# Recurrent sublayer: its recurrent columns projected first, the taps beside the other projections, the last operations tile by tile

## The reference, cut to what matters

```python
def rglru_block(h, w_in, conv_w, conv_b, w_r, b_r, w_i, b_i, lam, w_out):
    gate, xb = jnp.split(h @ w_in, 2, axis=-1)
    xp = jnp.pad(xb, ((0, 0), (CONV_W - 1, 0), (0, 0)))
    xc = conv_b + xp[:, 0:S] * conv_w[0]
    for tap in range(1, CONV_W):
        xc = xc + xp[:, tap:tap + S] * conv_w[tap]
    xblk = xc.reshape(B, S, LRU_BLOCKS, LRU_BLOCK_W)
    r = jax.nn.sigmoid(jnp.einsum('bsnk,nkj->bsnj', xblk, w_r).reshape(B, S, D_RNN) + b_r)
    i = jax.nn.sigmoid(jnp.einsum('bsnk,nkj->bsnj', xblk, w_i).reshape(B, S, D_RNN) + b_i)
    log_a = -LRU_C * r * jax.nn.softplus(-lam)
    a = jnp.exp(log_a)
    b = jnp.sqrt(-jnp.expm1(2.0 * log_a)) * (i * xc)
    _, hs = lax.associative_scan(_lin_rec_combine, (a, b), axis=1)
    y = jax.nn.gelu(gate) * hs
    return y @ w_out
```

## Time and profile before

| what | value |
|---|---|
| median of 3 runs | 2405.94 us (2405.05 to 2410.12) |
| profiled execution | 2406.02 us, its span 2404.4 us |
| PE busy | 2234.8 us, 93% of the span |
| PEld busy | 2038.2 us, 85% |
| DVE busy | 1634.5 us, 68% |
| ACT busy | 1216.3 us, 51% |
| POOL busy | 366.2 us, 15% |
| chain that ended last | PE 82%, DVE 7%, ACT 4%, issue 3%, DMA 3% |
| mean granted clock of PE | 0.96 |

### The profile page before, as it was taken

One profiled execution on the slowest core, in us unless ns is written; L12 is line 12 of the kernel. 1 busy time (PEld: TensorE's weight loads), 2 busy tenths in 40 slices (PEclk: granted clock), 3 DMA queues, 4 the chain that ended last, 5 costly groups with the idle time before them and its releaser, 6 DMA issues.

```text
span 2404.4 us, 37585 instructions
## 1 busy us (share of the span) xinstructions
PE 2234.8 (93%) x14486; PEld 2038.2 (85%) x14486; DVE 1634.5 (68%) x1943; ACT 1216.3 (51%) x1898; POOL 366.2 (15%) x513
## 2 busy tenths in 40 slices
PE   2999999999999994999998999998999699998998
PEld 2998987998899893899786998987988698877987
DVE  6767764767776846686787776775776776665654
ACT  2544545544553455553465554535544554565543
POOL 0111100111121103021101120800210121000210
PEclk9999989999999996999999999999999899999999
DMA  8788882688897961687765678512688378442562
GB/s 331 250 292 304 281 285 96 236 303 301 262 315 259 313 208 36 223 310 262 283 224 183 201 264 279 184 36 88 228 282 264 85 256 288 159 143 68 178 201 105
DMA packets 295522, 532.98 MB, mean 222 GB/s; under 512 B 10065, under 2 KB 185564, under 8 KB 295388
## 3 DMA queue, kind: packets, MB, share of 16 engines
q1 hardware_dynamic: 262396, 358.05, 45.3%
q0 software_dynamic: 32992, 173.09, 20.1%
HBM read 530.00 MB, written 1.11 MB: 221 GB/s over the span
## 4 chain that ended last, share of the span: by engine, by line
PE 82%; DVE 7%; ACT 4%; issue 3%; DMA 3%; SPq 0%; POOL 0%; DVEq 0%; ACTq 0%
PE bk L1344 12%; PE bk L1345 12%; PE bk L1346 12%; PE bk L1245 8%; PE bk L1243 8%; PE bk L1244 8%; PE bk L1395 3%; PE bk L1594 2%; DMA mod_raw<-in_ada_w 2%; DVE w_lo L1711 2%; PE bk L1288 1%; DVE mod_acc L1730 1%; PE bk L1231 1%; PE bk L1233 1%; PE bk L1232 1%
## 5 line engine op out<-in xcount | busy, mean ns | idle before, releaser
L1711 DVE TENSOR_TENSOR w_lo<-raw,w_hi 128x1024 fp32r<-128x1024 f32 (+5 forms) x720 | 833.0, 1185 | 512.7 <-ACT w_hi L791 511.4
L791 ACT ACTIVATE w_hi<-raw 128x1024 fp32r<-128x1024 f32 (+5 forms) x720 | 683.2, 976 | 683.0 <-PE bk L1245 335.7
L1344 PE MATMUL bk<-a_hi,w_hi 128*128 128x256 f32 x2332 | 664.5, 285 | 5.9 <-DVE a_lo L1796 5.9
L1345 PE MATMUL bk<-a_lo,w_hi 128*128 128x256 f32 x2332 | 663.0, 284 | 0.0
L1346 PE MATMUL bk<-a_hi,w_lo 128*128 128x256 f32 x2332 | 662.8, 284 | 0.0
L1344 PEld LDWEIGHTS bk<-a_hi,w_hi 128*128 128x128 f32 x2332 | 451.2, 194 | 7.1 <-DVE a_lo L1796 4.6
L1345 PEld LDWEIGHTS bk<-a_lo,w_hi 128*128 128x128 f32 x2332 | 451.1, 193 | 0.0
L1346 PEld LDWEIGHTS bk<-a_hi,w_lo 128*128 128x128 f32 x2332 | 450.9, 193 | 0.0
L1730 DVE SCALAR_TENSOR_TENSOR mod_acc<-mod_raw,cact,mod_acc 128x1536 f32<-128x1536 f32 x182 | 329.7, 1812 | 37.8 <-DMA mod_raw<-in_ada_w 22.8
L1245 PE MATMUL bk<-w_hi,hid_lo 128*128 128x512 f32 x832 | 327.5, 394 | 0.0
L1243 PE MATMUL bk<-w_hi,hid_hi 128*128 128x512 f32 x832 | 323.9, 389 | 3.7 <-DVE w_lo L1711 3.7
(11 more groups left out here) (341 smaller groups left out, 3180.6 us busy)
## 6 DMA issues: line engine op xcount, KB each, us to landing
raw<-in_ffn_w SPq DMA_DIRECT2D x128, 1024.0 KB, 5.5
mod_raw<-in_ada_w POOLq DMA_DIRECT2D x128, 768.0 KB, 6.1
raw<-in_ffn_w_gu SPq DMA_DIRECT2D x88, 1024.0 KB, 7.6
mod_raw<-in_mod_w POOLq DMA_DIRECT2D x80, 768.0 KB, 6.8
raw<-in_ffn_w_down SPq DMA_DIRECT2D x40, 1024.0 KB, 7.4
first_mod<-in_mod_w SPq DMA_DIRECT2D x16, 768.0 KB, 9.9
raw<-in_sb_w_qkv SPq DMA_DIRECT2D x12, 1024.0 KB, 7.1
raw<-in_conv_w_pw SPq DMA_DIRECT2D x12, 1024.0 KB, 5.4
```

The source lines that it names most:

```text
L791: ins = act.activation(o(w_hi[:, p % OPS, :]), r(raw[:, c % RAWS, :]), ACT.Copy)
L1344: pe.matmul(o, wh, a_hi[:, f, :], start=(f == 0), stop=False)
L1345: pe.matmul(o, wh, a_lo[:, f, :], start=False, stop=False)
L1711: ins = dve.tensor_tensor(o(w_lo[:, p % OPS, :]), r(raw[:, c % RAWS, :]), o(w_hi[:, p % OPS, :].bitcast(F32)), ALU.subtract)
```

## The change

Jobs 0 and 1 project recurrent tiles 0 to 7, job 2 gate tiles 0 and 1 and recurrent tiles 8 and 9, jobs 3 and 4 gate tiles 2 to 9. Job 2's two chunks take columns from two places, so each is loaded by two transfers of half the width; the first of each has a semaphore of its own (`mixed_landed`), for which ACT waits before it converts. The taps of DVE stand between the weight conversions of jobs 1, 2 and 3, in groups of four, four and two tiles. The gate matmuls begin in the banks of job 3, so the first four need not wait for ACT's eviction of job 4. The four last loops of DVE become one: round i makes product i, scan i - 1, Gelu product i - 2 and cast i - 3.

```diff
@@ -315,6 +315,7 @@
         prod_ready = sem("prod_ready")
         pos_landed = sem("pos_landed")
         pool_landed = sem("pool_landed")
+        mixed_landed = [sem("mixed_landed0"), sem("mixed_landed1")]
         pos_ready = sem("pos_ready")
         rope_read = sem("rope_read")
         rope_in = sem("rope_in")
@@ -380,6 +381,7 @@
             stages = stages[:stop]
         LAST_GROUP = max([0] + [h for z in stages for h in z["groups"]])
         st_pool = [z for z in stages if z["kind"] == "pool"]
+        st_lru = [z for z in stages if z["kind"] == "lru"]
         NPIECE = 2 * (stages[-1]["c"] + CHUNKS[stages[-1]["kind"]])
 
         act_base = [KD * (z["n"] + sum(y["kind"] == "conv" for y in stages[:z["n"]])) for z in stages]
@@ -541,7 +543,16 @@
                         plain(c + 12 + b, t["sb_w_o"][0], 4 * (b % 2), 4, 512 * (b // 2))
                 elif st["kind"] == "lru":
                     for b in range(10):
-                        plain(c + b, t["lru_w_in"][0], 4 * (b % 2), 4, b // 2 * 512)
+                        if b // 2 == 2:
+                            kt = 4 * (b % 2)
+                            sp.wait_ge(lo_ready, 2 * (c + b) + 2)
+                            for s in range(2):
+                                sp.dma_start(raw[:, (c + b) % RAWS, :].rearrange("p (k s m) -> p s k m", s=2, m=256)[:, s],
+                                             t["lru_w_in"][0][(b - 4) * 4 * P:(b - 3) * 4 * P, 2304 * s:2304 * s + 256]
+                                             .rearrange("(k p) m -> p k m", p=P))\
+                                    .then_inc(landed[(c + b) % RAWS] if s else mixed_landed[b - 4], 16)
+                        else:
+                            plain(c + b, t["lru_w_in"][0], 4 * (b % 2), 4, (1280, 1792, None, 256, 768)[b // 2])
                         if b == 1:
                             is_done(sp, c)
                             for g, name in enumerate(("lru_w_r", "lru_w_i")):
@@ -787,6 +798,9 @@
                     act.wait_ge(landed[c % RAWS], 16 * (c // RAWS + 1) + 16 * i)
                     if st_pool and p == 2 * st_pool[0]["c"]:
                         act.wait_ge(pool_landed, 16)
+                    for z in st_lru:
+                        if p in (2 * z["c"] + 8, 2 * z["c"] + 10):
+                            act.wait_ge(mixed_landed[p // 2 - z["c"] - 4], 16)
                     for o, r in split(p):
                         ins = act.activation(o(w_hi[:, p % OPS, :]), r(raw[:, c % RAWS, :]), ACT.Copy)
                     ins.then_inc(hi_ready, 2 if p in double else 1)
@@ -1163,18 +1177,18 @@
                     for b in range(5):
                         pieces(p + 4 + 4 * b, p + 8 + 4 * b)
                         is_done(act, c + 2 + 2 * b)
-                        first = 4 * b
-                        for a, e, f in ((first, min(first + 4, NB), 0), (max(first, NB), first + 4, 1)):
-                            if a >= e:
-                                continue
-                            bks = job_banks(w + b)[:, a - first:e - first, :]
-                            if f:
-                                ins = act.activation(lxb[:, a - NB:e - NB, TAPS - 1:], bks, ACT.Copy)
-                            else:
-                                ins = act.activation(lg[:, a:e, :], bks, ACT.Gelu_apprx_tanh)
+                        banks = job_banks(w + b)
+                        x_tiles, at = ((0, 4), 0) if b == 0 else ((4, 8), 0) if b == 1 else ((8, 10), 2) if b == 2 else ((0, 0), 0)
+                        g_tiles = ((0, 0), (0, 0), (0, 2), (2, 6), (6, 10))[b]
+                        if g_tiles[1]:
+                            ins = act.activation(lg[:, g_tiles[0]:g_tiles[1], :], banks[:, 0:g_tiles[1] - g_tiles[0], :],
+                                                 ACT.Gelu_apprx_tanh)
+                        if x_tiles[1]:
+                            ins = act.activation(lxb[:, x_tiles[0]:x_tiles[1], TAPS - 1:], banks[:, at:at + x_tiles[1] - x_tiles[0], :],
+                                                 ACT.Copy)
                         ins.then_inc(bank_free[(w + b) % 2], 1)
 
-                        for n in range(max(first - NB, 0), first + 4 - NB):
+                        for n in range(*x_tiles):
                             if n == 0:
                                 act.wait_ge(xb_zero, 1)
                             is_read(act, w + b)
@@ -1182,8 +1196,9 @@
                                            bias=col("lru_conv_b", n), scale=col("lru_conv_w", n)).then_inc(xc_first, 1)
                     for n in range(NB):
                         act.wait_ge(ri_done, n + 1)
-                        act.activation(lri[:, n, 0, :], bk[:, n % 8, 0:S], ACT.Sigmoid, bias=col("lru_b_r", n))
-                        act.activation(lri[:, n, 1, :], bk[:, n % 8, S:2 * S], ACT.Sigmoid, bias=col("lru_b_i", n))\
+                        ri = bk[:, (4 * ((w + 3) % 2) + n) % 8, :]
+                        act.activation(lri[:, n, 0, :], ri[:, 0:S], ACT.Sigmoid, bias=col("lru_b_r", n))
+                        act.activation(lri[:, n, 1, :], ri[:, S:2 * S], ACT.Sigmoid, bias=col("lru_b_i", n))\
                             .then_inc(ri_ready, 1)
                     for n in range(NB):
                         act.wait_ge(ri_ready, n + 1)
@@ -1671,14 +1686,16 @@
                         job(c + 2 * b, w + b, 0, A, 0, KD, first_in if b == 0 else None, by_feature(w, nq) if b == 0 else None)
                         turned()
                     is_read(pe, w + 3)
-                    is_read(pe, w + 4)
                     pe.wait_ge(lw_landed, 32)
                     for n in range(NB):
+                        if n == 4:
+                            is_read(pe, w + 4)
                         pe.wait_ge(xc_ready, n + 1)
                         if n >= 8:
                             pe.wait_ge(ri_ready, n - 7)
-                        pe.matmul(bk[:, n % 8, 0:S], lw[:, n, :], lxc[:, n, :], start=True, stop=True)
-                        pe.matmul(bk[:, n % 8, S:2 * S], lw[:, NB + n, :], lxc[:, n, :], start=True, stop=True)\
+                        ri = bk[:, (4 * ((w + 3) % 2) + n) % 8, :]
+                        pe.matmul(ri[:, 0:S], lw[:, n, :], lxc[:, n, :], start=True, stop=True)
+                        pe.matmul(ri[:, S:2 * S], lw[:, NB + n, :], lxc[:, n, :], start=True, stop=True)\
                             .then_inc(ri_done, 1)
                     pe.wait_ge(ri_ready, NB)
                     job(c + 10, w + 5, 0, A, 0, NB, lambda f: (lact_ready, f + 1), by_token(w + 5))
@@ -2201,22 +2218,29 @@
                     second_half(g, w + 7, c + 16)
                     pieces(p + 34, p + 35)
                 elif st["kind"] == "lru":
-                    pieces(p + 4, p + 24)
                     step = {}
-                    for a in range(0, NB, 2):
-                        for tap in range(1, TAPS):
-                            for n in range(a, a + 2):
-                                if tap == 1:
-                                    dve.wait_ge(xc_first, n + 1)
-                                else:
-                                    own_wait(step[n])
-                                ins = dve.scalar_tensor_tensor(out=lxc[:, n, :], in0=lxb[:, n, tap:tap + S],
-                                                               scalar=col("lru_conv_w", 10 * tap + n), in1=lxc[:, n, :],
-                                                               op0=ALU.mult, op1=ALU.add)
-                                if tap < TAPS - 1:
-                                    step[n] = own(ins)
-                                else:
-                                    ins.then_inc(xc_ready, 1)
+
+                    def later_taps(ns, tap):
+
+                        for n in ns:
+                            if tap == 1:
+                                dve.wait_ge(xc_first, n + 1)
+                            else:
+                                own_wait(step[n])
+                            ins = dve.scalar_tensor_tensor(out=lxc[:, n, :], in0=lxb[:, n, tap:tap + S],
+                                                           scalar=col("lru_conv_w", 10 * tap + n), in1=lxc[:, n, :],
+                                                           op0=ALU.mult, op1=ALU.add)
+                            if tap < TAPS - 1:
+                                step[n] = own(ins)
+                            else:
+                                ins.then_inc(xc_ready, 1)
+
+                    for b in range(5):
+                        ns = ((), range(0, 4), range(4, 8), range(8, 10), ())[b]
+                        for h in range(4):
+                            pieces(p + 4 + 4 * b + h, p + 5 + 4 * b + h)
+                            if h:
+                                later_taps(ns, h)
                     for n in range(NB):
                         dve.wait_ge(a_ready, n + 1)
 
@@ -2225,20 +2249,25 @@
                         own_wait(step[n])
```

(33 more changed lines are left out.)

## The result

The changed kernel took 2392.28 us (median of 5 runs, 2386.84 to 2394.41), the kernel before 2405.94 us beside it. The medians lie 13.7 us apart (a quotient of 0.9943). The ratio that is given with the runs is 0.9928, interval 0.9914 to 0.9941; it is not the quotient of the medians, and would make the gain 17 us. The forecast was 2400.9 us, with a range of 2391.0 to 2402.6; the median lies in the range, but by either measure the gain is far above the 5.1 us that were forecast. Rival A, which had 0.16, is what the profile shows.

The account below looks back on a forecast made before the run. PE was taken as busy almost throughout, so only its pauses in the recurrent sublayer could give time: 2406.0 - 4.8 (front) - 0.3 (last part) = 2400.9 us, range 2391 to 2402.6.

Parts of the forecast that it names:

- Rival A: Recurrent sublayer's last part: POOL gets in between DVE operations; 12.2 to 15.1 us with the front, 2391 to 2394; chance 0.16.
- So I take the first: Last part: POOL's first low part waits until DVE's forty operations end, so the joined loop adds only 0.3 us.
- such a row: An unbroken row of DVE operations, like 18 two-input ones during which POOL's L765 operation got nothing until the end.
- two or three operations: Joined last loop: each DVE operation depends on one two or three ahead; nothing charged for the waits.
- S': Start of DVE's last stretch of forty operations, forecast at 929.85 in place of 934.65.
- The late conversion: Within Rival A: DVE's next conversion comes some 3 us late for tile 8 of the output job, leaving 7.4 us.
- Its reason "against": Objection to Rival A: in earlier cases where POOL had turns, DVE's next operation was itself still waiting for a semaphore.
- The front: Projection order, taps beside jobs and gate matmul banks: the tenth Sigmoid begins at 915.86 in place of 920.68, 4.8 us earlier.
- From there a tile takes: Sigmoids on ACT after the first at 908.10: each tile was taken to need 0.8625 us.
- T: The last projection matmul, read as 904.80, where ACT's next conversion is released.
- The cover of the moved work: Gelu table load, taps, half-width transfers and POOL's L765 fit into idle time around the projection jobs; cost nothing.
- The clock: PE's granted clock in the output job after its long pause: no gain taken, 1 us allowed either way.

Follow-up runs that it names:

- pool_held: The changed kernel, but POOL waits for all ten casts before its first low part; 2400.44 us, ratio 0.9970.
- taps_mixed: The kernel before, but tap 2 is a plain addition with its convolution weight left out; POOL's first product took 1.55 us.
- front_only: The changed kernel with DVE's four last loops as in the kernel before; 2401.24 us, ratio 0.9978.
- taps_imm: The kernel before, but taps 1 to 3 multiply by the constant 0.5 instead of the weight column; POOL's record 5.82 us.
- taps_tt: The kernel before, but taps 1 to 3 are plain additions without convolution weights; POOL's record 6.48 us.
- taps_aligned: The kernel before, but all taps read the recurrent branch at offset 0, without the token shift; POOL's record 7.33 us.
- taps_fives: The kernel before, with taps in groups of five tiles in place of two; POOL's record 4.96 us.
- late_ix: The kernel before, but POOL's tenth L765 product waits for DVE's v step, so it asks beside DVE's plain products; POOL's record 3.46 us.
- late_wide: As late_ix, but DVE's first nine plain products are three operations of three tiles each; POOL's record 3.04 us.
- tail_only: The kernel before with only DVE's four last loops joined into one; 2396.85 us, ratio 0.9953.

## Why the prediction was wrong, point by point

**The step that failed** is "So I take the first: POOL stands until DVE has ended." The row of taps does hold POOL (7.33 us), and beside six further rows of one kind its record was 3.04 to 7.33 us long and ended 0.6 us behind the row (of the taps 16 were left when POOL's record began, not 18). The error was to call a row of products, scans, Gelu products and casts "such a row". In the rows I took for nearest all operations were of one kind, and this was what they had in common, while the new row changes its kind at every operation. The term was put at 0.3 us. Measured, PE starts 9.8 us earlier in the row and gives 2.05 back behind its start, so the term is 7.8 us. As a difference of whole stretches it is 7.3 (alone) to 8.4 us (on the front: 60.25 - 51.85), with the 0.48 and 0.67 us named above. The "two or three operations" between dependent ones hold only for the first rounds; later there are four between. This cost nothing: 14.63 us in `pool_held`.

**Rival A's working** held: PE at S' + 5.4 (5.85), rounds longer by 0.5 (0.54), DVE's end at S' + 20 (19.07). The late conversion was put at up to 3 us and cost 0.36, with 0.61 for one low part. Its reason "against", that DVE's operations in the earlier trace rows were still waiting for a semaphore, would not have told the two cases apart: in `taps_mixed` no tap waits for another engine from 904 to 914, and three of them took 2.68 us for 1.27 beside POOL's products. And the earlier trace rows held a change of kind as well: the long operation that ran when POOL asked was a plain TENSOR_TENSOR (L2122), the one behind it, ahead of which POOL had its turn, a SCALAR_TENSOR_TENSOR (L2126).

```profile
1871.71 1.83 DVE L2122 TENSOR_TENSOR pb<-pa 128x1614 f32<-128x1614 f32 x1
```

**The front** had the right mechanism and a term too small: 4.8 us for the tenth Sigmoid, 6.16 measured, and 6.0 at the start of DVE's row. The step "From there a tile takes (918.65 - 915.20)/4 = 0.8625 us" took the pace of the kernel before for ACT's. It was PE's: two gate matmuls of 0.43 us. After the change PE is ahead, and ACT goes at its own 0.716: nine tiles times 0.147 are 1.3 us. The rest held: banks, no pause ahead of the gate matmuls, table load (1.28 us, begun 1.99 us behind T), Gelu load (1.28 us) hidden in job 2.

**The cover of the moved work** held: PE is busy 57.00 of 57.4 us before T, and L776 (L765 before) has no record over 0.73 us, at no effect on the path.

**The clock** was allowed 1 us either way. In `front_only` and `pool_held` the same code runs between the first output matmul and the first square, and takes 20.80 and 20.14 us (20.13 before). The granted clock over that stretch was 0.86 in `front_only` and 0.89 in the other two: in the first 5 us it was 0.50 against 0.56, in the next 5 us 0.92 against 1.00. PE's pause ahead of it was 30.9 us there, 29.7 before and 31.7 in `pool_held`, so the length of the pause does not order them. That difference is not the change's, and its cause is open.

**The sum** would have been 2406.0 - 6.0 - 7.8 = 2392.2 us with these terms, and the median was 2392.28. The 13.7 us between the medians (12.5 for the changed kernel again) agree with the 13.8 found in the sublayer; that they agree to 0.1 us is luck, as single runs of one kernel lie up to 14 us apart and T varied by 10 us from trace to trace. The interval of the ratio, 14 to 21 us, lies wholly above 13.8; what would make up the rest is outside the sublayer and not shown, nor is what sets T.

## What to carry to other kernels

When you price a new row of operations by an old one, list what all operations of the old one have in common, and ask whether the new one shares it. A pace read while two engines follow each other belongs to the slower one; take it for the other only from a stretch where that one had work waiting. And where the runs spread more than the change is worth, measure between two points inside the stage: here these agreed within 0.02 us for one kernel, and within 0.7 for the same code in different kernels, while whole runs of one kernel differed by 14.

## What the runs showed of the hardware

These are readings of single traces of this kernel and its variants: the record of one POOL operation and DVE's row beside it. No rule beyond them is shown, and no cause.

| run | DVE's row | POOL's record, us | its end behind the row, us |
|---|---|---|---|
| before | 30 taps in 11.96 us | 7.33 | 0.59 |
| taps_imm | 30 taps with a constant in 10.14 us | 5.82 | 0.58 |
| taps_tt | 30 additions in 10.14 us | 6.48 | 0.59 |
| taps_aligned | 30 taps at offset 0 in 11.96 us | 7.33 | 0.58 |
| taps_fives | 30 taps in groups of five tiles in 11.96 us | 4.96 | 0.59 |
| late_ix | 9 products in 3.10 us | 3.46 | 0.58 |
| late_wide | 3 products of 768 elements in 2.69 us | 3.04 | 0.58 |
| taps_mixed | taps and additions by turns | 1.55 | ends inside the row |
| changed kernel, second low part | products, scans, Gelu products, casts | 0.84 | ends inside the row |

In `taps_mixed` three taps took 2.68 us for 1.27 behind POOL's first product. In the changed kernel a scan took 1.21 us for 0.69 beside a low part, the row 19.07 us for 14.63 in `pool_held`, and the two weight conversions behind the row 1.77 and 1.75 us for 1.23. POOL's transfer beside ten casts in a row took 1.65 us (before) and 1.64 us (`front_only`), and 0.60 us with one cast in a round (changed kernel, `tail_only`).
